# Expert stage of a diffusion step: a fourth split buffer for weights, laid in the token activations' tensors

## The chip, the core and the metric

The kernel runs on one core of a Trainium2 chip. The metric is the device time of one execution in microseconds (us). Five engines work side by side: TensorE (PE, matmuls), VectorE (DVE), ScalarE (ACT), GpSimd (POOL) and SyncE (SP, which issues most DMA transfers). They meet at semaphores.

## The reference, cut to what matters

The reference is one layer of a hybrid backbone on 640 tokens (128 of context, 512 latent) of width 1024. A mixer (a gated scan, differential attention and a merge) comes first; the change doesn't touch it. Then comes the expert stage, which is:

```
def ec_moe(h, router_w, w_gate, w_up, w_down):
    ...
    gate, idx = lax.top_k(jnp.swapaxes(aff, 1, 2), cap)
    ...
    a = jax.nn.silu(jnp.einsum('becd,edf->becf', xg, w_gate)) * jnp.einsum('becd,edf->becf', xg, w_up)
    y = jnp.einsum('becf,efd->becd', a, w_down) * gate[..., None].astype(h.dtype)
    return jnp.zeros_like(h).at[jnp.arange(B)[:, None], flat].add(y.reshape(B, N_EXPERTS * cap, D))
```

There are 16 experts. Each takes 80 tokens (64 latent and 16 of context) and three weight matrices of 1024 x 1024 in float32: gate, up and down. All weights are read once, 12.6 MB for an expert.

## The kernel before

To be exact enough, a product is made of three matmuls in a reduced float format (fp32r): both factors are split into a high part and a low part, and high x high, high x low and low x high are added (`mm3`, L1597 to L1601). ACT makes the high part by a copy with rounding, DVE the low part by a subtraction.

The expert stage runs from about 870 us to the end. Its weights come in pieces of 256 rows x 1024 columns, 1 MB, as 128 x 2048: four of gate, four of up and four of down for an expert, 192 in all, n = 0 to 191. The order is gate(e), up(e), down(e-1): the down product of an expert runs in the body of the next one. A piece goes through four steps:

- SP issues the transfer into one of six raw buffers (`eraw`, `NRE` = 6, `epiece`, L746). For piece n it waits until the low part of piece n-6 is made (`s_el`).
- ACT copies the raw piece into `Wh` (`ehi_first` L1067 at the start, `ehi_at` L1062 in the body, and again at the end, L1090). It waits for the landing (`s_er`) and for PE to be done with the piece that used the buffer before (`s_eu`). There are `NHL` = 3 buffers, so that is piece n-3. The body's step j handles piece n = 12e + j - 4.
- DVE makes `Wl` from the raw piece and `Wh` (`elo`, L1524).
- PE runs 12 matmuls on it, 80 rows of activations against 512 columns each (`piece_mm`, L1877), in the same order of pieces, and then raises `s_eu`.

Between the pieces other steps are written into each engine's program by hand, at fixed j. DVE: `alo` (low part of the hidden activations) after j = 3, `yout` (scaled output of the expert before) after 4, `xmod` (two operations on the gathered tokens) after 9, `xlo` (their low part) and `hidden` (silu(gate) x up) after 10. ACT: `ahi` after 3, `silu` after 7, `xhi` (high part of the gathered tokens) after 10. PE: transposition of the gathered tokens `turn_x` before 6, of the hidden ones `turn_a` after 11. POOL gathers the tokens of the next experts from HBM and scatters the outputs with an addition.

`act_hi` and `act_lo` are 128 x 8 x 640. They hold the split activations of all tokens for the layers ahead of the expert stage. In the expert stage slices 0, 1 and 2 of them hold the split activations of the experts (`xh`, `ah`, `xh1`); slices 3 to 7 are not used there.

Of the kernel before, what the change touches and what calls it, by code (L numbers as in the profile page):

```python
# [5 lines left out]
F32 = mybir.dt.float32  # L6
# [4 lines left out]
ALU = mybir.AluOpType  # L11
ACT = mybir.ActivationFunctionType
# [27 lines left out]
def fused_step(nc, A, outs):  # L40
# [8 lines left out]
    with ExitStack() as ctx:  # L49
# [155 lines left out]
        NRE = 6  # L205
        eraw = [part(0, 2048), part(2048, 2048), part(4096, 2048)] + raw
# [9 lines left out]
        brow = arena[:, o_vso + 2048:o_vso + 2560]  # L216
        yq = [v_hg, arena[:, o_vso + 2560:o_vso + 5120].rearrange("p (i n) -> p i n", i=NT)]
        kctx = yq[1][:, 0, :]

        xh, xl = (w[:, 0, :].rearrange("p (k t) -> p k t", k=KD) for w in (act_hi, act_lo))  # L220
        xh1, xl1 = (w[:, 2, :].rearrange("p (k t) -> p k t", k=KD) for w in (act_hi, act_lo))
# [636 lines left out]
        def _(act):  # L858
# [193 lines left out]
            def body(e, last=False):  # L1052
                for j in range(12):
                    ehi_at(e, j)
                    if j == 3:
                        ahi(e - 1)
                    if j == 7:
                        silu(e)
                    if j == 10 and not last:
                        xhi(e + 1)  # L1060

            def ehi_at(e, j):  # L1062
                act.wait_ge(s_er[(j + 2) % NRE], (e * 2 + (j - 4) // 6 + 1) * 16)
                act.wait_ge(s_eu, e * 12 + (j - 6))
                a.activation(Wh[(j + 2) % NHL], eraw[(j + 2) % NRE], ACT.Copy).then_inc(s_eh, 1)  # L1065

            def ehi_first(n):  # L1067
                act.wait_ge(s_er[n % NRE], 16 * (n // NRE + 1))
                if n >= NHL:
                    act.wait_ge(s_eu, n - 2)  # L1070
                a.activation(Wh[n % NHL], eraw[n % NRE], ACT.Copy).then_inc(s_eh, 1)

            filled(act, ("out", 1, NT - 1))
            for n in range(NHL):
                ehi_first(n)
            xhi(0)
            for n in range(NHL, 8):
                ehi_first(n)
                if n == 6:
                    act.wait_ge(s_eu, 4)  # L1080
                    a.activation(aa[0:CAP, :], pair(0)[0:CAP, :], ACT.Silu).then_inc(s_silu, 1)
# [4 lines left out]
            body(NE - 1, last=True)  # L1086
            for n in range(188, 192):
                act.wait_ge(s_er[n % NRE], 16 * (n // NRE + 1))
                act.wait_ge(s_eu, n - 2)
                a.activation(Wh[n % NHL], eraw[n % NRE], ACT.Copy).then_inc(s_eh, 1)  # L1090
                if n == 188:
                    ahi(NE - 1)

        @block.vector
        def _(dve):
# [427 lines left out]

            def elo(sl, ready, slot):  # L1524
                dve.wait_ge(s_eh, ready)
                v.tensor_tensor(Wl[sl], eraw[slot], Wh[sl].bitcast(F32), ALU.subtract).then_inc(s_el, 1)  # L1526

            def xmod(e):
                dve.wait_ge(s_xgT, e + 1)
# [24 lines left out]

            def body(e, first=False, second=False, last=False):
                for j in range(12):
                    elo((j + 2) % NHL, e * 12 + (j - 3), (j + 2) % NRE)
                    if j == 1 and first:
                        hidden(0, 8)
                    if j == 3:  # L1560
                        alo(e - 1)
                    if j == 4 and not first:
                        yout(e - 2, first=second)
                    if j == 9 and not last:
                        xmod(e + 1)
                    if j == 10:
                        if not last:
                            xlo(e + 1)
                        hidden(e, e * 12 + 4)

            for n in range(NHL):
                elo(n % NHL, n + 1, n % NRE)
            xmod(0)
            xlo(0)
            for n in range(NHL, 8):
                elo(n % NHL, n + 1, n % NRE)
                if n == 6:
                    xmod(1)
            xlo(1, (xh1, xl1))
# [2 lines left out]
            with dve.Fori(3, NE - 1) as e:  # L1582
                body(e)
            body(NE - 1, last=True)
            elo(188 % NHL, 189, 188 % NRE)
            alo(NE - 1)
            elo(189 % NHL, 190, 189 % NRE)
            yout(NE - 2)
            elo(190 % NHL, 191, 190 % NRE)
            elo(191 % NHL, 192, 191 % NRE)  # L1590
            yout(NE - 1)

        @block.tensor
        def _(pe):
# [282 lines left out]
            def piece_mm(pr, ready, sl, hi_, lo_, j):  # L1877

                pe.wait_ge(s_el, ready)
                wh, wl = (w[sl].rearrange("p (k n) -> p k n", k=2) for w in (Wh, Wl))  # L1880
# [13 lines left out]
            def body(e, first=False, last=False):  # L1894
                for j in range(12):
                    m, q = j // 4, j % 4
                    if j == 0:
                        pe.wait_ge(s_silu, e)
                    if j == 2 and first:
                        pe.wait_ge(s_xgm, 2)  # L1900
                        turn_a(0)
                    if j == 4:
                        pe.wait_ge(s_a, e)
                    if j == 6 and not last:
                        pe.wait_ge(s_alo, e)
                        turn_x(e + 1)
                    if j == 8:
                        pe.wait_ge(s_alo, e)
                        if not first:
                            pe.wait_ge(s_y, e - 1)  # L1910
                    hi_, lo_ = (ah, al) if m == 2 else (xh1, xl1) if first else (xh, xl)
                    if j == 0:
                        pe.wait_ge(s_xgl, e + 1)
                    piece_mm(m, e * 12 + (j - 3), (j + 2) % NHL, hi_, lo_, q)
                if not last:
                    pe.wait_ge(s_xgm, e + 2)
                turn_a(e)
# [2 lines left out]
            turn_x(0)  # L1920
            pe.wait_ge(s_xgl, 1)
            for n in range(8):
                piece_mm(n // 4, n + 1, n % NHL, xh, xl, n % 4)
                if n == 4:
                    pe.wait_ge(s_xgm, 1)
                    turn_x(1)
# [4 lines left out]
            pe.wait_ge(s_alo, NE)  # L1931
            pe.wait_ge(s_y, NE - 1)
            for q in range(4):
                piece_mm(2, 189 + q, (188 + q) % NHL, ah, al, q)


# [77 lines left out]
```

## Time and profile before

| | us |
|---|---|
| median of 3 runs | 1497.87 |
| lowest and highest | 1493.14 and 1497.9 |
| the profiled execution | 1495.61 |
| its span, first to last instruction | 1493.8 |

| engine | busy, us | share of the span |
|---|---|---|
| PE | 1346.1 | 90% |
| DVE | 1017.6 | 68% |
| ACT | 702.1 | 47% |
| POOL | 277.4 | 19% |

Over the whole span 296 MB are moved. The share of the sixteen DMA engines is low until about 870 us, and nine tenths or more in every slice of the expert stage but the last. Ends of matmuls are modelled in the profile, so starts are the better guide for PE: they are what the steps below use. A DMA share can be a little over 1, since packets on one engine overlap slightly.

### The profile page before, as it was taken

How to read it: one execution, taken by the hardware profiler on the slowest of the kernel's cores; microseconds unless marked ns; L12 is line 12 of the kernel's file. 1: busy time of each engine (PE TensorE's matmuls, PEld its weight loads, DVE VectorE, ACT ScalarE, POOL GpSimd, SP SyncE). 2: the span in 40 equal slices, each digit the busy share in tenths (PEclk: the TensorE clock that was granted, in tenths of full speed). 3: DMA queues.
4: the chain of work that ended last, by engine and by line, in shares of the span. 5: the costliest groups of instructions: out<-in, count | busy, mean ns of one | idle time of the engine just before them, and what ended most of it. 6: DMA issues, size and time to landing. Idle time of an engine off the chain costs nothing.

```text
span 1493.8 us, 18233 instructions
## 1 busy us (share of the span) xinstructions
PE 1346.1 (90%) x6820; PEld 1004.6 (67%) x6820; DVE 1017.6 (68%) x1093; ACT 702.1 (47%) x674; POOL 277.4 (19%) x193
## 2 busy tenths in 40 slices
PE   7788998888989978788999868999999999999995
PEld 1577887777979958684987725666666666666663
DVE  1766125444369868765443677899999898889993
ACT  2322234444335434314411125766667776767672
POOL 0022001111000000000000101144535335444222
PEclk9899999999989998878999878999999999999998
DMA  9412311113230121205415358999999999999992
GB/s 352 164 33 78 120 33 51 49 35 93 75 100 19 56 79 57 65 10 209 153 60 194 141 204 292 365 372 373 354 381 368 369 369 368 362 364 383 353 375 53
DMA packets 111843, 296.06 MB, mean 198 GB/s; under 512 B 7077, under 2 KB 33061, under 8 KB 111785
## 3 DMA queue, kind: packets, MB, share of 16 engines
q1 hardware_dynamic: 108264, 284.25, 52.4%
q0 software_dynamic: 3520, 11.01, 3.2%
q8 instruction: 39, 0.64, 0.2%
q14 instruction: 20, 0.16, 0.0%
HBM read 278.47 MB, written 16.78 MB: 198 GB/s over the span
## 4 chain that ended last, share of the span: by engine, by line
PE 67%; DVE 18%; issue 6%; ACT 6%; DMA 2%; POOL 1%; DVEq 0%; ACTq 0%; SPq 0%; POOLq 0%
PE ps L1599 17%; PE ps L1600 17%; PE ps L1601 17%; PE ps L1665 5%; PE ps L1775 3%; DVE w_lo L1526 3%; ACT w_hi L1065 2%; PE ps L1726 1%; ACT w_hi L876 1%; DVE arena L1542 1%; DMA arena<-in_w_mod_dram 1%; DVE arena L1166 1%; PE ps L1852 1%; DVE w_lo L1117 1%; DVE arena L1361 1%
## 5 line engine op out<-in xcount | busy, mean ns | idle before, releaser
L1526 DVE TENSOR_TENSOR w_lo<-arena,w_hi 128x2048 fp32r<-128x2048 f32 x192 | 435.3, 2287 | 65.1 <-ACT w_hi L1065 49.9
L1599 PE MATMUL ps<-w_hi,act_hi 128*80 128x512 f32 (+1 forms) x1048 | 418.9, 400 | 28.4 <-DVE w_lo L1526 15.0
L1600 PE MATMUL ps<-w_lo,act_hi 128*80 128x512 f32 (+1 forms) x1048 | 414.0, 395 | 0.0
L1601 PE MATMUL ps<-w_hi,act_lo 128*80 128x512 f32 (+1 forms) x1048 | 412.6, 394 | 0.0
L1065 ACT ACTIVATE w_hi<-arena 128x2048 fp32r<-128x2048 f32 x180 | 343.3, 1915 | 141.9 <-PE ps L1601 141.9
L1599 PEld LDWEIGHTS ps<-w_hi,act_hi 128*80 128x80 f32 (+1 forms) x1048 | 168.5, 161 | 115.3 <-DVE w_lo L1526 29.7
L1601 PEld LDWEIGHTS ps<-w_hi,act_lo 128*80 128x80 f32 (+1 forms) x1048 | 168.3, 161 | 75.4 <-issue 0.9
L1600 PEld LDWEIGHTS ps<-w_lo,act_hi 128*80 128x80 f32 (+1 forms) x1048 | 168.7, 161 | 68.6 <-issue 0.7
L1599 PE MATMUL ps<-act_hi,w_hi 128*128 128x320 f32 x576 | 190.6, 331 | 1.4 <-DVE w_lo L1117 0.7
L1600 PE MATMUL ps<-act_lo,w_hi 128*128 128x320 f32 x576 | 184.6, 321 | 0.0
L1601 PE MATMUL ps<-act_hi,w_lo 128*128 128x320 f32 x576 | 184.3, 320 | 0.0
L1117 DVE TENSOR_TENSOR w_lo<-arena,w_hi 128x2048 fp32r<-128x2048 f32 (+1 forms) x34 | 73.5, 2166 | 108.7 <-ACT w_hi L876 108.3
L880 ACT ACTIVATE arena<-ps 128x512 f32<-128x512 f32 (+3 forms) x84 | 51.4, 618 | 143.2 <-PE ps L1665 57.2
L1599 PEld LDWEIGHTS ps<-act_hi,w_hi 128*128 128x128 f32 x576 | 115.8, 201 | 3.7 <-issue 2.5
L839 POOL DMA_INDIRECT out_dram<-arena x16 | 73.1, 4567 | 228.3 <-DVE arena L1552 228.3
L1600 PEld LDWEIGHTS ps<-act_lo,w_hi 128*128 128x128 f32 x576 | 115.1, 200 | 0.0
L1601 PEld LDWEIGHTS ps<-act_hi,w_lo 128*128 128x128 f32 x576 | 114.2, 198 | 0.0
L1775 PE MATMUL ps<-arena 128*128 128x64 f32 x560 | 81.3, 311 | 33.6 <-DVE arena L1361 23.7
L793 POOL TENSOR_SCALAR arena<-arena 128x1 f32<-128x1 f32 (+2 forms) x44 | 9.8, 223 | 522.9 <-ACT arena L954 223.2
L1775 PEld LDWEIGHTS ps<-arena 128*128 128x128 f32 x560 | 79.4, 226 | 35.6 <-DVE arena L1361 24.6
L1665 PE MATMUL ps<-arena 128*2 128x512 f32 x192 | 90.6, 627 | 10.9 <-DMA arena<-in_w_mod_dram 10.1
L876 ACT ACTIVATE w_hi<-arena 128x2048 fp32r<-128x2048 f32 (+1 forms) x34 | 61.4, 1809 | 54.3 <-PE ps L1601 44.1
(199 smaller groups left out, 1351.1 us busy)
## 6 DMA issues: line engine op xcount, KB each, us to landing
arena<-in_w_exp_gate_dram SPq DMA_DIRECT2D x64, 1024.0 KB, 8.9
arena<-in_w_exp_up_dram SPq DMA_DIRECT2D x64, 1024.0 KB, 7.3
arena<-in_w_exp_down_dram SPq DMA_DIRECT2D x64, 1024.0 KB, 7.1
arena<-in_w_mod_dram SPq DMA_DIRECT2D x24, 1024.0 KB, 5.3
arena<-in_w_in_dram SPq DMA_DIRECT2D x18, 1024.0 KB, 5.3
arena<-in_w_in_dram SPq DMA_DIRECT2D x12, 512.0 KB, 5.5
gl_raw<-arena SPq DMA_DIRECT2D x32, 160.0 KB, 1.8
arena<-gl_raw SPq DMA_DIRECT2D x8, 640.0 KB, 10.2
```

What stands on the lines that cost most here:

```text
L839: g.indirect_dma_start(out=y_sample[0], out_offset=bass.IndirectOffsetOnAxis(ap=iscat[0:CAP_LAT, 0:1], axis=0), in_=ye[0:CAP_LAT, :], in_o ...
L876: a.activation(hl(key)[0][:, 0:w], rawv(key)[:, 0:w], ACT.Copy).then_inc(s_hi, 1)
L880: release(a.activation(dst, src, func, **kw), key)
L1065: a.activation(Wh[(j + 2) % NHL], eraw[(j + 2) % NRE], ACT.Copy).then_inc(s_eh, 1)
L1117: v.tensor_tensor(l_[:, 0:w], rawv(key)[:, 0:w], h_[:, 0:w].bitcast(F32), ALU.subtract).then_inc(s_lo, 1)
L1166: link(v.tensor_reduce(mx[:, m:m + 1], pair(m)[:, 0:nk], AX_X, ALU.max))
L1526: v.tensor_tensor(Wl[sl], eraw[slot], Wh[sl].bitcast(F32), ALU.subtract).then_inc(s_el, 1)
L1599: t.matmul(out, sh, mh, start=start, stop=False)
L1600: t.matmul(out, sh, ml, start=False, stop=False)
L1601: return t.matmul(out, sl, mh, start=False, stop=stop)
L1665: ins = t.matmul(bank(2 * modpair(j))[0:2, :], cond[:, kt, :], w[:, kk, :], start=kt == 0, stop=kt == 7)
L1775: ins = t.matmul(bank(4 + 2 * (lv % 2) + d)[:, 64 * c:64 * c + 64], KS[lv % 2][:, d, P * c:P * c + P], QC[lv % 2][:, d, 64 * c:64 * c + 64 ...
```

## The change

A fourth pair of split buffers is added for the expert stage. Its high part lies in slices 3 and on of `act_hi`, its low part in the same place of `act_lo`. The buffer of a piece is n modulo 4 instead of 3, and ACT waits for PE to be done with piece n-4 instead of n-3. To keep the order safe, `xhi` moves from step 10 to step 11 on ACT and `xlo` from step 10 to behind the split of step 11 on DVE. The layers ahead of the stage still use three buffers. Cut to its core:

```diff
+        NEW = 4
+        EWh, EWl = (ws + [a[:, 3:, :].rearrange("p k t -> p (k t)")[:, 0:2048]] for ws, a in ((Wh, act_hi), (Wl, act_lo)))
...
-                    if j == 10 and not last:
+                    if j == 11 and not last:
                         xhi(e + 1)
             def ehi_at(e, j):
                 act.wait_ge(s_er[(j + 2) % NRE], (e * 2 + (j - 4) // 6 + 1) * 16)
-                act.wait_ge(s_eu, e * 12 + (j - 6))
-                a.activation(Wh[(j + 2) % NHL], eraw[(j + 2) % NRE], ACT.Copy).then_inc(s_eh, 1)
+                act.wait_ge(s_eu, e * 12 + (j - 7))
+                a.activation(EWh[j % NEW], eraw[(j + 2) % NRE], ACT.Copy).then_inc(s_eh, 1)
             def ehi_first(n):
                 act.wait_ge(s_er[n % NRE], 16 * (n // NRE + 1))
-                if n >= NHL:
-                    act.wait_ge(s_eu, n - 2)
-                a.activation(Wh[n % NHL], eraw[n % NRE], ACT.Copy).then_inc(s_eh, 1)
+                if n >= NEW:
+                    act.wait_ge(s_eu, n - 3)
+                a.activation(EWh[n % NEW], eraw[n % NRE], ACT.Copy).then_inc(s_eh, 1)
...
             def body(e, first=False, second=False, last=False):
                 for j in range(12):
-                    elo((j + 2) % NHL, e * 12 + (j - 3), (j + 2) % NRE)
+                    elo(j % NEW, e * 12 + (j - 3), (j + 2) % NRE)
...
                     if j == 10:
-                        if not last:
-                            xlo(e + 1)
                         hidden(e, e * 12 + 4)
+                    if j == 11 and not last:
+                        xlo(e + 1)
...
-                    piece_mm(m, e * 12 + (j - 3), (j + 2) % NHL, hi_, lo_, q)
+                    piece_mm(m, e * 12 + (j - 3), j % NEW, hi_, lo_, q)
```

ACT at the start of the expert stage, before: the splits of pieces 0 to 5 and the high part of the first gathered tokens. The fourth split waits for PE (`s_eu`).

```order
L1071 ACTIVATE w_hi0<-arena 128x2048 [waits s_er0,psum_full2]
L1071 ACTIVATE w_hi1<-arena 128x2048 [waits s_er1]
L1071 ACTIVATE w_hi2<-arena 128x2048 [waits s_er2]
L1041 ACTIVATE act_hi<-arena 128x640 [waits s_xgf]
L1071 ACTIVATE w_hi0<-arena 128x2048 [waits s_eu,s_er3]
L1071 ACTIVATE w_hi1<-arena 128x2048 [waits s_eu,s_er4]
L1071 ACTIVATE w_hi2<-arena 128x2048 [waits s_eu,s_er5]
```

The same place with the change; `act_hi` with 128x2048 is the fourth buffer.

```order
L1074 ACTIVATE w_hi0<-arena 128x2048 [waits s_er0,psum_full2]
L1074 ACTIVATE w_hi1<-arena 128x2048 [waits s_er1]
L1074 ACTIVATE w_hi2<-arena 128x2048 [waits s_er2]
L1044 ACTIVATE act_hi<-arena 128x640 [waits s_xgf]
L1074 ACTIVATE act_hi<-arena 128x2048 [waits s_er3]
L1074 ACTIVATE w_hi0<-arena 128x2048 [waits s_eu,s_er4]
L1074 ACTIVATE w_hi1<-arena 128x2048 [waits s_eu,s_er5]
```

The fourth split now waits for its landing alone; from the fifth on each waits for PE, one piece further back than before.

DVE in the body of expert 2, steps 8 to 11, before: splits, `xmod` (the two rows on `arena` 128x640), `xlo` and `hidden` (80x1024).

```order
L1526 TENSOR_TENSOR w_lo1<-arena,w_hi1 128x2048 [waits s_eh]
L1526 TENSOR_TENSOR w_lo2<-arena,w_hi2 128x2048 [waits s_eh]
L1530 TENSOR_TENSOR arena<-ps,arena 128x640 [waits s_xgT]
L1532 TENSOR_TENSOR arena<-arena 128x640 [waits s_xgm]
L1526 TENSOR_TENSOR w_lo0<-arena,w_hi0 128x2048 [waits s_eh,s_xgf]
L1537 TENSOR_TENSOR act_lo<-arena,act_hi 128x640 [waits s_xgh]
L1542 TENSOR_TENSOR arena<-arena,ps 80x1024 [waits s_eu,s_silu]
L1526 TENSOR_TENSOR w_lo1<-arena,w_hi1 128x2048 [waits s_eh]
```

The same place with the change.

```order
L1529 TENSOR_TENSOR w_lo0<-arena,w_hi0 128x2048 [waits s_eh]
L1529 TENSOR_TENSOR w_lo1<-arena,w_hi1 128x2048 [waits s_eh]
L1533 TENSOR_TENSOR arena<-ps,arena 128x640 [waits s_xgT]
L1535 TENSOR_TENSOR arena<-arena 128x640 [waits s_xgm]
L1529 TENSOR_TENSOR w_lo2<-arena,w_hi2 128x2048 [waits s_eh,s_xgf]
L1545 TENSOR_TENSOR arena<-arena,ps 80x1024 [waits s_eu,s_silu]
L1529 TENSOR_TENSOR act_lo<-arena,act_hi 128x2048 [waits s_eh]
L1540 TENSOR_TENSOR act_lo<-arena,act_hi 128x640 [waits s_xgh]
```

The low part of the gathered tokens (128x640) moved from ahead of `hidden` to behind the last split.

## Rows read from the trace of the kernel before

**Rows 1.** List of waits from 900 us on: engine, line, releaser, us, times, longest.

```profile
ACT w_hi L1065 <- PE ps L1601: 141.9, 135, 2.2
PE ps L1599 <- DVE w_lo L1526: 15.0, 15, 1.1
```

**Rows 2.** Timeline of PE in one expert: start, duration, engine, line, operation, idle before.

```profile
1098.53 0.39 PE L1601 MATMUL ps<-w_hi,act_lo 128*80 128x512 f32 x1
1099.02 0.47 PE L1599 MATMUL ps<-w_hi,act_hi 128*80 128x512 f32 x1
...
1101.39 0.39 PE L1600 MATMUL ps<-w_lo,act_hi 128*80 128x512 f32 x1
1101.62 0.40 PE L1601 MATMUL ps<-w_hi,act_lo 128*80 128x512 f32 x1
1103.09 0.46 PE L1599 MATMUL ps<-w_hi,act_hi 128*80 128x512 f32 x1 [1.07 <-DVE w_lo L1526]
```

**Rows 3.** Timeline of DVE over the same stretch.

```profile
1092.67 2.29 DVE L1526 TENSOR_TENSOR w_lo<-arena,w_hi 128x2048 fp32r<-128x2048 f32 x1 [1.03 <-ACT w_hi L1065]
1094.88 0.82 DVE L1530 TENSOR_TENSOR arena<-ps,arena 128x640 f32<-128x640 f32 x1
1095.73 0.83 DVE L1532 TENSOR_TENSOR arena<-arena 128x640 f32<-128x640 f32 x1
1096.68 2.29 DVE L1526 TENSOR_TENSOR w_lo<-arena,w_hi 128x2048 fp32r<-128x2048 f32 x1
1098.88 0.82 DVE L1537 TENSOR_TENSOR act_lo<-arena,act_hi 128x640 fp32r<-128x640 f32 x1
1099.62 1.21 DVE L1542 TENSOR_TENSOR arena<-arena,ps 80x1024 f32<-80x1024 f32 x1
1100.75 6.68 DVE L1526 TENSOR_TENSOR w_lo<-arena,w_hi 128x2048 fp32r<-128x2048 f32 x3
```

**Rows 4.** Timeline of ACT at the start of the stage.

```profile
901.01 0.74 ACT L1041 ACTIVATE act_hi<-arena 128x640 fp32r<-128x640 f32 x1 [6.21 <-DVE arena L1532]
907.12 1.91 ACT L1071 ACTIVATE w_hi<-arena 128x2048 fp32r<-128x2048 f32 x1 [5.37 <-PE ps L1601]
```

**Rows 5.** Stretches: length, busy PE, PEld, DVE, ACT, POOL, PE clock, DMA share, GB/s.

```profile
905.00:914.00 9.00, 9.00 (x40) 5.79 (x39) 4.46 (x2) 5.19 (x3) 0.00 (x0) 0.97 0.20 50
1122.36:1158.19 35.83, 34.68 (x162) 22.19 (x161) 32.31 (x18) 24.92 (x16) 17.77 (x7) 1.00 1.01 371
1167.00:1172.00 5.00, 4.85 (x22) 2.91 (x21) 4.84 (x5) 3.78 (x4) 3.28 (x4) 1.00 1.03 422
1464.00:1476.00 12.00, 7.13 (x25) 4.52 (x26) 6.58 (x5) 4.97 (x3) 4.02 (x2) 0.72 0.20 27
```

**Rows 6.** DMA queues and issues, 943.2 to 1444.8 (14 experts): share; us to landing.

```profile
q1 hardware_dynamic: 45729, 176.29, 93.8%
q0 software_dynamic: 2704, 8.52, 7.3%
...
arena<-in_w_exp_down_dram SPq DMA_DIRECT2D x57, 1024.0 KB, 7.1
arena<-in_w_exp_gate_dram SPq DMA_DIRECT2D x56, 1024.0 KB, 9.0
```

**Rows 7.** DMA queues, 874 to 882, weights alone: packets, MB, share.

```profile
q1 hardware_dynamic: 918, 3.31, 102.9%
```

**Rows 8.** The transfer of piece 9 on SP's queue: issue, and time to landing.

```profile
L748 SPq DMA_DIRECT2D arena<-in_w_exp_gate_dram x1: 383/383/383, 911.5 to 911.5; - x1
...
DMA to landing us min/median/max: 4.8/4.8/4.8
```

**Rows 9.** The transfer of piece 187, the same view.

```profile
L748 SPq DMA_DIRECT2D arena<-in_w_exp_down_dram x1: 373/373/373, 1442.7 to 1442.7; - x1
...
DMA to landing us min/median/max: 6.0/6.0/6.0
```

**Rows 10.** Timeline of PE: first matmul of piece 187, and of piece 188.

```profile
1459.26 0.39 PE L1599 MATMUL ps<-w_hi,act_hi 128*80 128x512 f32 x1
...
1468.87 0.69 PE L1599 MATMUL ps<-w_hi,act_hi 128*80 128x512 f32 x1 [6.16 <-issue]
```

More of the change, by code:

```diff
@@ L1063, in ehi_at @@
                 act.wait_ge(s_er[(j + 2) % NRE], (e * 2 + (j - 4) // 6 + 1) * 16)
-                act.wait_ge(s_eu, e * 12 + (j - 6))
-                a.activation(Wh[(j + 2) % NHL], eraw[(j + 2) % NRE], ACT.Copy).then_inc(s_eh, 1)
+                act.wait_ge(s_eu, e * 12 + (j - 7))
+                a.activation(EWh[j % NEW], eraw[(j + 2) % NRE], ACT.Copy).then_inc(s_eh, 1)
             def ehi_first(n):
                 act.wait_ge(s_er[n % NRE], 16 * (n // NRE + 1))
-                if n >= NHL:
-                    act.wait_ge(s_eu, n - 2)
-                a.activation(Wh[n % NHL], eraw[n % NRE], ACT.Copy).then_inc(s_eh, 1)
+                if n >= NEW:
+                    act.wait_ge(s_eu, n - 3)
+                a.activation(EWh[n % NEW], eraw[n % NRE], ACT.Copy).then_inc(s_eh, 1)
             filled(act, ("out", 1, NT - 1))
-            for n in range(NHL):
+            for n in range(3):
                 ehi_first(n)
             xhi(0)
-            for n in range(NHL, 8):
+            for n in range(3, 8):
                 ehi_first(n)
@@ L1088, in _ @@
                 act.wait_ge(s_er[n % NRE], 16 * (n // NRE + 1))
-                act.wait_ge(s_eu, n - 2)
-                a.activation(Wh[n % NHL], eraw[n % NRE], ACT.Copy).then_inc(s_eh, 1)
+                act.wait_ge(s_eu, n - 3)
+                a.activation(EWh[n % NEW], eraw[n % NRE], ACT.Copy).then_inc(s_eh, 1)
                 if n == 188:
@@ L1525, in elo @@
                 dve.wait_ge(s_eh, ready)
-                v.tensor_tensor(Wl[sl], eraw[slot], Wh[sl].bitcast(F32), ALU.subtract).then_inc(s_el, 1)
+                v.tensor_tensor(EWl[sl], eraw[slot], EWh[sl].bitcast(F32), ALU.subtract).then_inc(s_el, 1)
             def xmod(e):
@@ L1566, in body @@
                     if j == 10:
-                        if not last:
-                            xlo(e + 1)
                         hidden(e, e * 12 + 4)
-            for n in range(NHL):
-                elo(n % NHL, n + 1, n % NRE)
+                    if j == 11 and not last:
+                        xlo(e + 1)
+            for n in range(3):
+                elo(n % NEW, n + 1, n % NRE)
             xmod(0)
             xlo(0)
-            for n in range(NHL, 8):
-                elo(n % NHL, n + 1, n % NRE)
+            for n in range(3, 8):
+                elo(n % NEW, n + 1, n % NRE)
                 if n == 6:
@@ L1584, in _ @@
             body(NE - 1, last=True)
-            elo(188 % NHL, 189, 188 % NRE)
+            elo(188 % NEW, 189, 188 % NRE)
             alo(NE - 1)
-            elo(189 % NHL, 190, 189 % NRE)
+            elo(189 % NEW, 190, 189 % NRE)
             yout(NE - 2)
-            elo(190 % NHL, 191, 190 % NRE)
-            elo(191 % NHL, 192, 191 % NRE)
+            elo(190 % NEW, 191, 190 % NRE)
+            elo(191 % NEW, 192, 191 % NRE)
             yout(NE - 1)
@@ L1879, in piece_mm @@
                 pe.wait_ge(s_el, ready)
-                wh, wl = (w[sl].rearrange("p (k n) -> p k n", k=2) for w in (Wh, Wl))
+                wh, wl = (w[sl].rearrange("p (k n) -> p k n", k=2) for w in (EWh, EWl))
                 for kk in range(2):
@@ L1922, in _ @@
             for n in range(8):
-                piece_mm(n // 4, n + 1, n % NHL, xh, xl, n % 4)
+                piece_mm(n // 4, n + 1, n % NEW, xh, xl, n % 4)
                 if n == 4:
@@ L1933, in _ @@
             for q in range(4):
-                piece_mm(2, 189 + q, (188 + q) % NHL, ah, al, q)
+                piece_mm(2, 189 + q, (188 + q) % NEW, ah, al, q)
 _INS = ['x_prompt', 'x_sample', 'cache_v', 'state_hgrn', 'w_mod', 'b_mod', 'w_in', 'diff_lambda', 'w_branch_hgrn', 'w_branch_attn', 'w_out', 'router_w', 'w_exp_gate', 'w_exp_up', 'w_exp_down']
```

## The prediction

> **What bounds the kernel now.** I read the list of waits first, then the timelines of TensorE (PE), VectorE (DVE) and ScalarE (ACT) in one expert, then the DMA shares, because the edit touches only the expert stage. A piece below is 1 MB of expert weights (256 x 1024), numbered n = 0 to 191, twelve to an expert.
>
> The waits [rows 1] say that ACT's split waits for PE 135 times, 141.9 us in all: it wants a buffer that PE still reads. That is idle time of an engine with time to spare. What counts is the other row: PE's first matmul of a piece waited for DVE's low part 15 times, 15.0 us, longest 1.1. Fourteen of these are one hole per expert. [Rows 2] show it: matmuls start 0.23 us apart (1101.39, 1101.62), then the next at 1103.09, which is 1.47 - 0.23 = 1.24 us lost. One piece earlier the step is 0.49 (1098.53 to 1099.02), 0.26 lost. So a hole costs 1.24 + 0.26 = **1.50 us per expert**.
>
> [Rows 3] show who is late. DVE has between three splits of 2.2 to 2.3 us each the gather's modulation (0.82 + 0.83), the low part of the activations (0.82) and the hidden product (1.21), some 3.5 us. PE takes 2.75 us for a piece. With three buffers ACT may start piece n when PE ends n-3, two pieces before it is wanted: 2 x 2.75 = 5.5 us, of which ACT's 1.91 [rows 4] and DVE's 2.29 take 4.2. The lead is 1.3 us, and the burst eats it.
>
> One expert lasts 35.83 us (the window of [rows 5]), so PE alone could do it in 35.83 - 1.50 = **34.33**. DVE is busy 32.31 of it, ACT 24.92.
>
> The third thing to see is the DMA. In that window its share is 1.01 at 371 GB/s; over 14 experts, 501.6 us, the two queues took 93.8% + 7.3% = 101.1% of 16 engines [rows 6]. Where weights alone stream with a full queue, the share is 102.9% [rows 7] and the rate 422 GB/s [rows 5]. So the engines are idle only (102.9 - 101.1)/102.9 = 1.75% of the time, 0.63 us of an expert. Gathers and scatters take the rest. **The DMA can't do an expert in less than about 35.20 us.** That is the term that decides the size here: the hole is 1.50, but only 0.63 of it can be had for ever.
>
> **The change part by part.**
>
> Fourth buffer. ACT may start n when PE ends n-4; the lead is 1.3 + 2.75 = 4.0 us. The burst needs about 3.5 less what DVE gains per piece (2.75 - 2.2, twice), 2.4 at most. The hole goes: at most 14 x 1.50 = 21.0 us. The number of splits, matmuls and transfers is unchanged. The transfers' ring of six raw buffers is the same too, but each transfer is issued when a low part is done, so it goes out up to one piece earlier.
>
> Low part of the activations moved behind the last split of the expert (0.82 us), on ACT its high part likewise. It leaves the path to the late split; the next reader is PE's first piece of the next expert, behind one more piece and a transposition. The cover is over 2.75 us. I count nothing extra, it is within the 1.50. If the cover were gone it would cost 0.8 per expert.
>
> Start of the stage. ACT is free at 901.01 + 0.74 = 901.75 and then waits 5.37 us for PE, until 907.12 [rows 4]. Piece 3 now needs no such wait: its low part ends at 901.75 + 1.91 + 2.29 = 906.0, and the transfer of piece 9 goes out then rather than at 911.5 [rows 8]. The DMA is nearly idle here (share 0.20 from 905 to 914 [rows 5]). Piece 4 still waits for PE's first piece at 907.12 and is done about 911.4, where piece 3 was. So from there all transfers are one piece ahead: the DMA has **2.5 us** of work done sooner (1 MB at 422 GB/s [rows 5]). PE itself gains nothing here.
>
> DMA idle. With one more piece queued its pauses should close: 14 x 0.63 = **8.8 us** at most, zero at least.
>
> Stock. Weights land earlier than needed today. Piece 187, the last ahead of the closing four, was issued at 1442.7, landed 6.0 us later at 1448.7 [rows 9], and PE began it at 1459.26 [rows 10]: 10.55 us. The least is 1.91 + 2.29 + 0.1 for hand-offs, 4.3, plus up to 1.2 for the hidden product in front and about 0.6 for uneven landings, 6.0. PE can move **4.5 us** (3.5 to 6.2) towards the landings before it must wait for them.
>
> Tail. After piece 187 PE waits 6.16 us [rows 10] for the scaled output of the expert before, which DVE makes after a split that ACT starts only after the last activations' high part. That order is unchanged, so nothing there: 0.
>
> Buffer 4 lies in another tensor. No row shows a split or a matmul on it. Splits of the same shape into the three others take 1.91 and 2.29; I take the same and 0 for it. The nearest row on that tensor is the 128x640 copy into `act_hi`, 0.74 us [rows 4]; scaled by columns that would be 2.4 for a split, 0.5 more on every fourth piece. ACT, busy 24.92 of 35.83, hides that, and less than nothing isn't to be had where the engines are not the bound.
>
> **Sum.** 2.5 + 8.8 + 4.5 = **15.8 us**, below the 21.0 of PE, so DMA decides. Against the profiled execution's 1495.61 (span 1493.8) that is 1479.8; against the median 1497.87, 1482.1. I say 1482. Seen in time: PE gains 1.50 an expert while DMA gives 0.63, so the stock of 2.5 + 4.5 lasts 7.0/0.87 = 8 experts, and the last six come at 35.2.
>
> **Rivals.**
>
> *DMA keeps up with PE.* If its share can rise further, or gathers and scatters cost less when hidden, the whole 21 goes: 1497.9 - 21 = 1477. For it: no wait for a landing appears in [rows 1]. Against it: the share of 1.01.
>
> *DMA gives no more than today.* If the 1.75% can't be closed, since a piece lands only when the slowest of 16 engines is done, only 2.5 + 4.5 = 7 is left: 1491. For it: the queue already holds more than one transfer most of the time (7.1 to 9.0 us to land [rows 6] against 4.8 for a lone one [rows 8]).
> The Trainium skill, page DMA: Bandwidth & Descriptors, section Where 436 GB/s comes from, speaks for this rival: it says that loads from HBM are bound near 358 GB/s a core and that the vendor's model uses 368. By that figure the present 371 would be the ceiling and the last two terms of this rival's case the whole gain; the trace differs from it with 422 in a quiet stretch, so I don't take it.
>
> *The buffer doesn't help.* The burst is DVE's own and DVE is at 32.31 of 34.33 us. If hand-offs add 2 us an expert, DVE is the bound and the hole only moves: 1498, within 0.3%. Against: DVE's gaps outside the burst all end on ACT.
>
> *Slower: the clock.* Once DMA decides, PE waits in lumps behind the scatters and gathers. After 1.07 us idle the granted clock stayed 1.00 [rows 2, 5]; after 6.16 it was 0.72 over 12 us [rows 5, 10]. That is half level (1.2 instead of 2.4 GHz) for 0.28/0.5 x 12 = 6.7 us, 4.9 of them idle, so at least 0.9 us lost by a fall, 2.7 (a whole piece at half speed) at most. Two falls an expert at 1.8 make 34.33 + 3.6 = 37.9, 2.1 above today: 1498 + 14 x 2.1 = 1527. It decides from where falls cost more than the 1.50 of the hole. Lumps of more than about 3 us would be needed, and a scatter delays a landing by some 2.
>
> **How the numbers follow.** Forecast (DMA-bound, 13 to 19 gained) 52%; DMA keeps up 16%; DMA as today 18%; no help 9%; slower 5%. The range takes in the first three, with 3 us below and above for the spread of the medians (1493.1 to 1497.9): 1474 to 1493. About 4.5 us, 0.3%, is what a measurement can tell from no change. Faster than that: 52 + 16 + 15 of the 18 = 83%; same 12%; slower 5%.
>
> **What would show it.** The row of PE waiting for DVE's low part once per expert is gone in the first experts. The expert period is near 34.4 first and 35.2 later. ACT's split waits for the DMA in the later half, which it never does now. DMA share goes from 1.01 to about 1.03, GB/s from 371 to about 378. Piece 9 is issued at about 906. The 6.16 us before the last four pieces stays. I am wrong if the period is 34.4 to the end, if it stays near 35.8 with the holes elsewhere, or if the PE clock falls inside the stage.

## The result, and the profile after

The changed kernel takes 1471.45 us in the median of 4 runs (1469.97 to 1473.77). The kernel before, run beside it, takes 1495.64 (1493.14 to 1497.9). The ratio is 0.9843, with a 95% interval of 0.983 to 0.9856. That is faster, as forecast, but by 10 us more than the 1482 of the prediction, and below the low end of its range, 1474. The profiled execution took 1470.25 with a span of 1468.4; before it was 1495.61 and 1493.8. So 25.4 us are to be found.

First the list of waits of PE from 900 us on, after (engine, line, releaser, us in total, times, longest). The row of [rows 1] in which PE waited 15 times for DVE's low part has no successor.

```profile
PE ps L1602 <- issue: 6.2, 1, 6.2
PE ps L1602 <- DVE act_lo L1540: 3.5, 1, 3.5
```

Of the other engines in the same view of after, ACT waits for PE less long than the 141.9 us of [rows 1] (94.0 + 36.2, split over the two kinds of buffer). No row has ACT waiting for a weight's landing.

```profile
ACT w_hi L1068 <- PE ps L1604: 94.0, 114, 1.4
...
ACT act_hi L1068 <- PE ps L1604: 36.2, 44, 0.9
DVE w_lo L1529 <- ACT w_hi L1068: 17.5, 43, 1.0
```

The period of an expert tells the rest. Two stretches of one expert each, after, in the columns of [rows 5] (length, busy PE, PEld, DVE, ACT, POOL, PE clock, DMA share, GB/s):

```profile
972.50:1006.66 34.16, 34.16 (x162) 22.39 (x161) 32.31 (x18) 25.04 (x16) 20.44 (x7) 1.00 1.03 394
1040.82:1074.98 34.16, 34.16 (x162) 22.39 (x161) 32.31 (x18) 25.04 (x16) 20.20 (x7) 1.00 1.02 385
```

PE is busy for the whole of both. The period is 34.16 us from the first repeated expert to the last, against 35.83 before, so 1.67 less, and 14 of these make 23.4 us. DVE's and ACT's work is what it was, 32.31 and 25.04 (24.92). The DMA moves the same bytes in less time, at 385 to 394 GB/s where it was 371.

The DMA queues of after over 14 experts (packets, MB, share of 16 engines), and the median time to landing, against [rows 6]:

```profile
q1 hardware_dynamic: 45896, 176.97, 94.8%
q0 software_dynamic: 2704, 8.52, 7.6%
...
arena<-in_w_exp_down_dram SPq DMA_DIRECT2D x58, 1024.0 KB, 7.7
arena<-in_w_exp_gate_dram SPq DMA_DIRECT2D x56, 1024.0 KB, 8.8
```

Start and end of the stage on PE's timeline. The first row is of before; the others are of after and answer to [rows 10].

```profile
902.73 0.72 PE L1599 MATMUL ps<-w_hi,act_hi 128*80 128x512 f32 x1 [3.47 <-DVE act_lo L1537]
```

```profile
900.82 0.71 PE L1602 MATMUL ps<-w_hi,act_hi 128*80 128x512 f32 x1 [3.47 <-DVE act_lo L1540]
...
1436.64 0.72 PE L1894 MATMUL ps<-arena 80*128 80x80 f32 x8
1443.52 0.68 PE L1602 MATMUL ps<-w_hi,act_hi 128*80 128x512 f32 x1 [6.16 <-issue]
```

The whole account closes on these rows. From the first piece to piece 188 it was 1468.87 - 902.73 = 566.14 us, and is 1443.52 - 900.82 = 542.70: 23.4 less. The stage starts 1.9 us earlier, and that is spread and no effect of the change: in the thirteen traces on record this first matmul starts anywhere from 900.47 (experiment 3) to 904.26 (experiment 6). From piece 188 to the end it is 24.88 after and 24.93 before. 23.4 + 1.9 + 0.05 = 25.4.

### The profile page after: what moved, and what is told of

It is laid out like the page before. It is cut to its first block, busy times and chain, and to the rows that moved or that the text cites. A ratio compares the mean times of both kernels' runs of the same rounds, so it can differ in the third digit from the quotient of the medians.

```text
span 1468.4 us, 18232 instructions
## 1 busy us (share of the span) xinstructions
PE 1336.2 (91%) x6820; PEld 1005.8 (68%) x6820; DVE 1017.2 (69%) x1093; ACT 702.9 (48%) x674; POOL 339.7 (23%) x193
## 4 chain that ended last, share of the span: by engine, by line
PE 78%; DVE 12%; ACT 4%; issue 3%; DMA 2%; POOL 1%; DVEq 0%; ACTq 0%; SPq 0%; POOLq 0%
PE ps L1602 21%; PE ps L1603 20%; PE ps L1604 20%; PE ps L1668 5%; PE ps L1778 4%; ACT w_hi L879 1%; PE ps L1729 1%; DMA arena<-in_w_mod_dram 1%; DVE arena L1169 1%; PE ps L1855 1%; DVE w_lo L1120 1%; DVE arena L1364 1%; DVE arena L1363 1%; ACT arena L883 1%; DVE arena L1220 1%
## 5 line engine op out<-in xcount | busy, mean ns | idle before, releaser
L1602 PE MATMUL ps<-w_hi,act_hi 128*80 128x512 f32 (+1 forms) x856 | 341.6, 399 | 12.0 <-issue 6.2
L1529 DVE TENSOR_TENSOR w_lo<-arena,w_hi 128x2048 fp32r<-128x2048 f32 x144 | 325.4, 2286 | 24.4 <-ACT w_hi L1068 17.5
L1603 PE MATMUL ps<-w_lo,act_hi 128*80 128x512 f32 (+1 forms) x856 | 338.8, 396 | 0.0
L1604 PE MATMUL ps<-w_hi,act_lo 128*80 128x512 f32 (+1 forms) x856 | 337.4, 394 | 0.0
L1068 ACT ACTIVATE w_hi<-arena 128x2048 fp32r<-128x2048 f32 x135 | 258.5, 1918 | 94.0 <-PE ps L1604 94.0
L1602 PEld LDWEIGHTS ps<-w_hi,act_hi 128*80 128x80 f32 (+1 forms) x856 | 140.2, 164 | 71.6 <-issue 8.6
L1604 PEld LDWEIGHTS ps<-w_hi,act_lo 128*80 128x80 f32 (+1 forms) x856 | 139.8, 163 | 59.6 <-issue 0.7
L1603 PEld LDWEIGHTS ps<-w_lo,act_hi 128*80 128x80 f32 (+1 forms) x856 | 140.3, 164 | 55.7 <-issue 0.7
L1529 DVE TENSOR_TENSOR act_lo<-arena,act_hi 128x2048 fp32r<-128x2048 f32 x48 | 109.8, 2288 | 8.3 <-ACT act_hi L1068 6.1
L1778 PE MATMUL ps<-arena 128*128 128x64 f32 x560 | 81.3, 311 | 33.6 <-DVE arena L1364 23.7
L1068 ACT ACTIVATE act_hi<-arena 128x2048 fp32r<-128x2048 f32 x45 | 86.3, 1918 | 36.2 <-PE ps L1604 36.2
```

The source lines that it names most:

```text
L1068: a.activation(EWh[j % NEW], eraw[(j + 2) % NRE], ACT.Copy).then_inc(s_eh, 1)
L1529: v.tensor_tensor(EWl[sl], eraw[slot], EWh[sl].bitcast(F32), ALU.subtract).then_inc(s_el, 1)
L1602: t.matmul(out, sh, mh, start=start, stop=False)
L1603: t.matmul(out, sh, ml, start=False, stop=False)
L1604: return t.matmul(out, sl, mh, start=False, stop=stop)
L1778: ins = t.matmul(bank(4 + 2 * (lv % 2) + d)[:, 64 * c:64 * c + 64], KS[lv % 2][:, d, P * c:P * c + P], QC[lv % 2][:, d, 64 * c:64 * c + 64 ...
```

## The experiments

**1. The order alone, with three buffers.** The gathered tokens' split moved behind the last one, the fourth buffer left out. Against the changed kernel:

```diff
-        NEW = 4
-        EWh, EWl = (ws + [a[:, 3:, :].rearrange("p k t -> p (k t)")[:, 0:2048]] for ws, a in ((Wh, act_hi), (Wl, act_lo)))
...
-                act.wait_ge(s_eu, e * 12 + (j - 7))
-                a.activation(EWh[j % NEW], eraw[(j + 2) % NRE], ACT.Copy).then_inc(s_eh, 1)
+                act.wait_ge(s_eu, e * 12 + (j - 6))
+                a.activation(Wh[(j + 2) % NHL], eraw[(j + 2) % NRE], ACT.Copy).then_inc(s_eh, 1)
```

> Three split buffers as before, but the order of the change: the high part of the gathered tokens at step 11 on ScalarE, their low part behind the last split on VectorE. Theory L (the hole is VectorE's burst less the lead of the split buffers, and nothing else limits): the burst shrinks by the 0.74 us of the low part, so the expert takes 35.83 - 0.74 = 35.1 us and the kernel gains 14 x 0.74 = 10 us. Rival M (the gain of the change comes from transfers going out a piece earlier): nothing is issued earlier here, so gain near 0.

Measured: 1483.7 us, ratio 0.9924 (0.9909 to 0.9939), period 35.07. PE's wait for the low part and the window of one expert:

```profile
PE ps L1599 <- DVE w_lo L1526: 4.6, 14, 0.3
```

```profile
1048.90:1083.90 35.00, 34.57 (x161) 22.23 (x160) 32.15 (x19) 25.02 (x16) 19.98 (x7) 1.00 1.01 376
```

The gain is 10.9 us where theory L had 10. The holes are still 14, but of 0.3 us each instead of 1.07. Taking 0.82 us of DVE work out of the burst gives 0.76 of the 1.67 us per expert. So with three buffers the moved low part is worth nearly half of what the change brought, and the prediction had named no price for it apart from the buffer.

**2. Four buffers, old order.** The split of the gathered tokens back to its old place, with a wait that keeps the shared tensor safe:

```diff
-                    if j == 11 and not last:
+                    if j == 10 and not last:
+                        act.wait_ge(s_eu, e * 12 + 4)
```

> Four split buffers, with the order of before (high part of the gathered tokens at step 10, with a wait of its own for TensorE's step 7, and their low part ahead of the hidden product). Theory L: the lead is 1.3 + 2.75 = 4.0 us against a burst that cost 2.9 to 3.0 (lead 1.3 plus hole 1.67), so no hole: expert 34.16 us, the same time as the changed kernel, ratio 0.984 to before. Rival O (the new order matters as well): an expert between 34.2 and 34.9.

Measured: 1472.17, ratio 0.9843 (0.9827 to 0.9858), the same as the change. Its window of one expert:

```profile
1042.00:1076.16 34.16, 34.16 (x162) 22.39 (x161) 32.31 (x19) 25.05 (x15) 20.37 (x7) 1.00 1.03 391
```

This is theory L again. The buffer by itself closes the hole, and the order then adds nothing. The two parts of the change are two cures for one burst; their gains don't add.

**3. A longer burst.** Two more DVE operations on 128x640 (0.82 us each) per expert, behind the hidden product. They write to slices that nothing reads.

```diff
+                        for w in (act_lo, act_hi):
+                            v.tensor_tensor(w[:, 7, :].rearrange("p (k t) -> p k t", k=KD), xgt3, xgt3, ALU.subtract)
```

> The changed kernel with two more VectorE operations of 128x640 (about 0.8 us each, results unused) between the hidden product and the last split of each expert. Theory L: the lead has 4.0 - (2.97 - 0.74) = 1.8 us to spare, the addition is 1.5 to 1.65, VectorE's load rises from 32.3 to 33.9 of 34.16: no or hardly any hole (under 0.2 us), ratio 0.984 to 0.986. Rival V (VectorE as a whole becomes the bound, hand-offs included): expert over 34.5 us, ratio 0.988 or more.

Measured: 1526.16, ratio 1.0221 (1.0191 to 1.025), so 55 us slower than the change for some 25 us of added DVE work. This was a clear miss, and none of my theories had a place for it. Most experts still take 33.6 to 35.0 us, but five of them take 43.2 to 46.4. What these five and the expert behind each take above 34.16 adds up to 54.6 us, nearly the whole loss. PE's wait in those is not for DVE but for the gather:

```profile
PE ps L1879 <- DMA arena<-xn_rows,arena: 43.7, 5, 9.7
```

These waits are 43.7 us of the loss. Most of the rest is the clock: behind each wait the matmuls of 512 columns take 0.63 us for a time instead of 0.39.

The gather is late because of POOL, which ahead of each indirect DMA copies a column of indices (80, 64 and 16 numbers). POOL's timeline in one bad expert, and DVE's at its end:

```profile
1066.19 24.30 POOL L837 COPY arena<-arena 64x1 uint32 x1
1090.44 0.18 POOL L838 COPY arena<-arena 16x1 uint32 x1
...
1101.84 22.80 POOL L831 COPY arena<-arena 80x1 uint32 x1 [5.14 <-DMA out_dram<-arena]
```

```profile
1083.76 4.48 DVE L1529 TENSOR_TENSOR w_lo<-arena,w_hi 128x2048 fp32r<-128x2048 f32 x2
1088.16 2.28 DVE L1529 TENSOR_TENSOR act_lo<-arena,act_hi 128x2048 fp32r<-128x2048 f32 x1
1090.49 2.29 DVE L1529 TENSOR_TENSOR w_lo<-arena,w_hi 128x2048 fp32r<-128x2048 f32 x1
```

A copy of 64 numbers took 24.30 us and ended when DVE ended: 1088.16 + 2.28 = 1090.44. From 1066.4 to there each DVE instruction begins before the recorded end of the one before; the first gap is 1090.44 to 1090.49. Then the copy of 16 numbers takes 0.18 us. Four of the five late gathers stand behind a copy at L831 of 22.6 to 22.8 us that ends at such a gap. The fifth doesn't: its copy took 1.91 us, and the indirect DMA instruction itself was slow.

```profile
1292.94 25.01 POOL L826 DMA_INDIRECT arena<-xn_rows,arena  x1 [0.85 <-POOL arena L831]
```

I overlooked that row before experiment 4. Experiments 4 and 5 test this reading. In experiment 7, where DVE has little to do, no copy of L831 takes more than 0.18:

```profile
L831 POOL COPY arena<-arena x15: 177/180/181, 898.5 to 1335.4; 80x1 uint32 x13, 80x1 uint32<-80x1 uint32 x2
```

**4. The same burst without the index copies.** The indirect DMAs read their column of the index table directly, in a POOL loop written out:

```diff
-                g.tensor_copy(icur[0:CAP, 0:1], iT[0:CAP, bass.ds(e, 1)]).then_inc(s_icp, 1)
-                pool.wait_ge(s_icp, e + 1)
...
-                                     in_offset=bass.IndirectOffsetOnAxis(ap=icur[0:CAP, 0:1], axis=0)).then_inc(s_gath, 16)
+                                     in_offset=bass.IndirectOffsetOnAxis(ap=iT[0:CAP, e:e + 1], axis=0)).then_inc(s_gath, 16)
```

> The kernel e3_burst_plus (two more VectorE operations per expert) without GpSimd's copies of the indices: its loop over experts is written out, and each gather and scatter takes its index column directly. Theory G (GpSimd's small copy can't finish while VectorE runs without a gap; the gather then goes out up to 24 us late and TensorE waits for it, five times 10 us): without the copies no wait for a gather is left and the time falls from 1526 to about 1472 to 1478 (expert 34.2 to 34.5). Rival V (VectorE's load as such, 33.9 of 34.16 us, is the cause): the time stays above 1510.

Measured: 1487.01 in the median of 10 runs, nine of them from 1481.46 to 1494.5 and one at 1511.93; ratio of the nine 0.9946 (0.9924 to 0.9968). Against experiment 3 that is 39 us back, and waits for the gather fall from five to one. In the profiled execution (1482.41) the rest is the same delay at another place. POOL's timeline, and a window of 350 us of the same kernel:

```profile
988.59 23.66 POOL L826 DMA_INDIRECT arena<-xn_rows,arena  x1 [4.94 <-DMA out_dram<-arena]
```

```profile
1040.00:1390.00 350.00, 350.00 (x1638) 229.31 (x1637) 342.94 (x205) 256.33 (x155) 107.28 (x30) 1.00 1.02 386
```

Here the indirect DMA instruction itself took 23.66 us, as the one at 1292.94 in experiment 3; the other fifteen gathers of this kernel take 0.90 to 2.11. It costs one expert 10.0 us, and the stage starts 2.0 later than in the profiled execution of the change: 12.0 of the 12.2 us between them. The window shows DVE busy 98% with no hole on PE at all: DVE's load as such is not what cost the time. The expectation of full recovery was wrong by 9 to 15 us. Whether the slower of the ten executions held more such delays isn't shown, since only one was profiled.

The Trainium skill, page SBUF — State Buffer, section SBUF: two separate sides, says that a VectorE instruction with two SBUF inputs and a GpSimd instruction that reads SBUF share a pair of ports as an exclusive lock, held for the whole instruction by whoever starts first. The direction agrees. The trace of experiment 3 shows more than one instruction's worth: the copy of 24.30 us stood through some fifteen DVE instructions in a row, two of which (L1549, L1555) take one input from PSUM, and was let in at a gap of 0.05 us.

**5. One added operation instead of two.**

> The changed kernel with one more VectorE operation (0.74 to 0.82 us) per expert in place of two, GpSimd's copies kept. Asks how near the edge the changed kernel is: VectorE still has gaps adding up to about 1.0 us an expert. Theory G: some gap is left after the burst, copies take 10 to 20 us but the gather still lands before TensorE wants it (it has 18 to 21 us to spare): ratio to before 0.984 to 0.986. If the copies already miss every gap: over 0.99.

Measured: 1471.04, ratio 0.9833 (0.9817 to 0.985), the same as the change. The copies at L837 now take up to 12.8 us where in the change they take up to 9.9, and before up to 7.7. The row of before, of after, and of this run (duration in ns: least, median, most):

```profile
L834 POOL COPY arena<-arena x16: 193/1942/7689, 949.3 to 1476.3; 64x1 uint32 x13, 64x1 uint32<-64x1 uint32 x3
```

```profile
L837 POOL COPY arena<-arena x16: 180/1576/9890, 947.7 to 1453.0; 64x1 uint32 x13, 64x1 uint32<-64x1 uint32 x3
```

```profile
L837 POOL COPY arena<-arena x16: 177/1819/12829, 949.4 to 1454.8; 64x1 uint32 x13, 64x1 uint32<-64x1 uint32 x3
```

The longest copy of 16 numbers, at L838, goes from 0.8 (before) and 10.7 (the change) to 13.7. PE waits for none of them yet. These copies end otherwise than in experiment 3. The one of 13.65 us ends at 1068.09, with the end of a DVE split (1068.06) and without a gap behind it; ten more do the same at this place.

```profile
1054.44 13.65 POOL L838 COPY arena<-arena 16x1 uint32 x1
```

```profile
1065.78 2.28 DVE L1529 TENSOR_TENSOR act_lo<-arena,act_hi 128x2048 fp32r<-128x2048 f32 x1
1067.98 0.81 DVE L1549 TENSOR_TENSOR act_lo<-ps,act_hi 128x640 fp32r<-128x640 f32 x1
```

So a recorded gap is not the only way in. Why the copies of experiment 3 stood through the same place stays open.

The edge lies between one and two added operations. With one, DVE is busy 32.87 us of 34.16 and nothing is lost; with two it is 33.47 (342.94 of 350 in the window of experiment 4) and the time is. The change itself stands between one and two such operations from it. In its trace one gather had already become late: the indirect DMA instruction took 10.61 us, and 7.3 us were left before PE wanted the tokens, where the gathers of the other experts from the fourth on leave 18 to 21.

**6 to 8. The floor of the DMA.** To see what an expert costs when PE and DVE have little to do, only the high x high matmuls remain (a third of them), and DVE subtracts a quarter of each piece. Against the change (the same edit on the kernel before gives experiment 6):

```diff
-                v.tensor_tensor(EWl[sl], eraw[slot], EWh[sl].bitcast(F32), ALU.subtract).then_inc(s_el, 1)
+                v.tensor_tensor(EWl[sl][:, 0:512], eraw[slot][:, 0:512], EWh[sl][:, 0:512].bitcast(F32), ALU.subtract).then_inc(s_el, 1)
...
-                        ins = mm3(bank(2 * pr + b)[0:CAP, :], (hi_[:, kt, :], lo_[:, kt, :]), (wh[:, kk, cs], wl[:, kk, cs]), kt == 0, kt == 7)
+                        ins = t.matmul(bank(2 * pr + b)[0:CAP, :], hi_[:, kt, :], wh[:, kk, cs], start=kt == 0, stop=kt == 7)
```

Experiment 6, three buffers:

> The kernel before (three buffers), with computation left out so that the transfers are what remains: TensorE multiplies high by high only (a third of the expert matmuls) and VectorE subtracts a quarter of each piece. All transfers, gathers and scatters stay. Theory D (as predicted: the DMA needs 35.2 us for an expert): the expert stays at 35.2 or more. Theory P (packet time is elastic, the share of 1.01 is no bound): the expert falls below 34.16, to between 30.5 (12 pieces at 2.54) and 33.5, and the DMA is then the bound.

Experiment 7, four buffers:

> The changed kernel with the same computation left out as in the run before. If the fourth buffer changes how fast the DMA can go, the expert is shorter than there; if the DMA's floor doesn't depend on it, both have the same period within 0.3 us. Theory D: 35.2 in both. Theory P: 30.5 to 33.5 in both.

Experiment 8, as 7 but without the two scatters of an expert and the waits for them (DVE's and SP's waits go too, and aren't shown):

```diff
-                g.indirect_dma_start(out=y_sample[0], out_offset=bass.IndirectOffsetOnAxis(ap=iscat[0:CAP_LAT, 0:1], axis=0),
-                                     in_=ye[0:CAP_LAT, :], in_offset=None, compute_op=ALU.add).then_inc(s_scat, 16)
...
-                pool.wait_ge(s_scat, 32 * e + 32)
```

> As the run before, and the scatters of the experts' outputs are left out too (32 transfers). Gathers stay. The period falls by what the two scatters of an expert cost the weight transfers. From the trace before, landings beside scatters come about 2.5 us later than otherwise: expected 2 to 2.6 us less than the run before, and a DMA rate near 410 GB/s.

Measured, one run each: 1441.2, 1437.56 and 1409.73 us, with periods of 33.57, 33.57 and 32.17. The queues of the three kernels from 940 to 1360 us, in that order:

```profile
q1 hardware_dynamic: 40911, 157.74, 94.9%
q0 software_dynamic: 2538, 7.97, 7.9%
```

```profile
q1 hardware_dynamic: 40946, 157.87, 95.0%
q0 software_dynamic: 2496, 7.87, 7.8%
```

```profile
q1 hardware_dynamic: 42742, 164.79, 99.5%
q0 software_dynamic: 1152, 3.93, 3.2%
```

Here the DMA is the bound: now ACT's splits do wait for landings (first row, experiment 7), and DVE is far from full in the window of one expert (second).

```profile
ACT w_hi L1068 <- DMA arena<-in_w_exp_gate_dram: 31.4, 40, 1.4
```

```profile
1100.00:1133.57 33.57, 22.65 (x66) 11.04 (x65) 13.68 (x18) 24.95 (x15) 4.53 (x6) 0.65 1.03 394
```

So the floor is 33.57 us per expert with three buffers or with four, where the prediction had 35.20 and theory P, just missed, at most 33.5. PE at 34.16 lies above it by 0.59, and PE decides. The scatters cost 33.57 - 32.17 = 1.4 us per expert of DMA time; I had expected 2 to 2.6, and 410 GB/s where 402 came.

**9. The tail.** The 6.16 us before piece 188 had been counted as unchanged. In this version the scaled output of the expert before, and the split of piece 189, stand ahead of the last activations' split:

```diff
-                if n == 188:
+                if n == 189:
...
-            alo(NE - 1)
...
+            alo(NE - 1)
```

> The changed kernel with another order at the end: VectorE makes the scaled output of expert 14 before the low part of the last activations, and ScalarE splits piece 189 before their high part. TensorE waits 6.16 us ahead of the last four pieces today. Expected: this falls to about 2 us (scaled output 1.3, low part 0.8), and the slow start after it (4.33 us for a piece instead of 2.75) may go too: 4 to 6 us less than the changed kernel, ratio to before 0.980 to 0.9815. Rival: something else ends last there, a gain under 1 us.

Measured: 1467.04, ratio 0.9811 (0.9798 to 0.9825), as expected. PE's wait falls from 6.16 to 1.65:

```profile
1438.15 0.72 PE L1894 MATMUL ps<-arena 80*128 80x80 f32 x8
1440.52 0.46 PE L1602 MATMUL ps<-w_hi,act_hi 128*80 128x512 f32 x1 [1.65 <-DVE act_lo L1549]
1440.82 0.46 PE L1603 MATMUL ps<-w_lo,act_hi 128*80 128x512 f32 x1
1441.08 0.63 PE L1604 MATMUL ps<-w_hi,act_lo 128*80 128x512 f32 x1
```

The matmuls still slow down, from 0.39 to 0.63 us, after a wait of only 1.65 that follows eight small transpositions. (In experiment 11 they don't, after the same wait.)

**10. The tail, with PE kept at work.** Experiment 9 with eight matmuls of 512 columns, whose result nothing reads, between the transpositions and piece 188:

```diff
+            for q in range(8):
+                t.matmul(bank(0)[0:CAP, :], xh[:, q, :], act_hi[:, 7, 0:512], start=q == 0, stop=q == 7)
```

> e4_tail with eight more matmuls of 512 columns on TensorE (result unused, 1.8 us in all) between the last transposition and the last four pieces, where it is idle for 1.86 us and where the first of the four pieces then takes 4.4 us instead of 2.75. If the idle time is what lowers the granted clock there: the piece takes 2.75 us and the kernel gains 1.5 us on e4_tail, ratio to before near 0.980. Rival: the clock falls anyway, same time as e4_tail or 0.1 us more.

Measured: 1466.19 (1464.81 to 1466.49), ratio 0.9803 (0.979 to 0.9816). The stretch of 12 us in after, experiment 9 and this one:

```profile
1437.00:1449.00 12.00, 5.84 (x24) 3.66 (x22) 8.71 (x5) 6.10 (x4) 4.79 (x1) 0.72 0.00 0
```

```profile
1437.00:1449.00 12.00, 10.35 (x44) 6.60 (x43) 6.74 (x5) 4.30 (x3) 4.47 (x4) 0.86 0.21 27
```

```profile
1437.00:1449.00 12.00, 12.00 (x59) 7.85 (x58) 7.39 (x5) 4.31 (x3) 4.47 (x4) 1.00 0.21 27
```

The granted clock stays 1.00 and piece 188 takes 2.8 us instead of 4.4. From its first matmul to the end of the span it is 23.5 us instead of 25.2. The median gains only 0.85 us over experiment 9, within both intervals, so in the time it is not settled. That the added matmuls are the cause isn't shown either: the clock stays up without them in experiment 11. It is the fastest of the kernels that compute everything.

**11. The tail without index copies.** Experiment 9 together with the edit of experiment 4.

> e4_tail and no index copies on GpSimd. The copies take up to 10.7 us there but the gathers land 18 to 21 us before they are wanted, so nothing waits for them: same time as e4_tail, ratio to before 0.981 within its interval, perhaps 0.3 us at the very end, where a scatter's copies stand ahead of the scatter. Rival: indirect transfers themselves are slower with a strided index column, which would show as a longer GpSimd instruction but not in the time.

Measured: 1467.22, ratio 0.9809 (0.9794 to 0.9824), the same as experiment 9. In this kernel the copies cost nothing. Its trace bears on experiments 9 and 10: PE waits the same 1.65 us behind the same transpositions, with nothing put in, and the granted clock stays 1.00.

```profile
1441.76 0.46 PE L1593 MATMUL ps<-w_hi,act_hi 128*80 128x512 f32 x1 [1.65 <-DVE act_lo L1540]
1442.06 0.39 PE L1594 MATMUL ps<-w_lo,act_hi 128*80 128x512 f32 x1
```

```profile
1437.00:1449.00 12.00, 10.35 (x52) 6.76 (x51) 7.98 (x5) 4.31 (x3) 4.20 (x2) 1.00 0.22 27
```

From piece 188 to the end it is 23.4 us here, as in experiment 10. In both profiled executions the stretch from piece 0 to piece 188 is 1.4 us longer than in experiment 9, so the whole time hardly shows it.

## Why the prediction was wrong

**The hole.** Right in kind: it was the short lead over DVE's burst, as experiments 1 and 2 show from both sides. One reading was loose: the steps between DVE's splits add up to 0.82 + 0.83 + 0.82 + 1.21 = 3.68 us, not 3.5, which leaves the need (2.6 with it) below the lead of 4.0 all the same. The hole's size was put at 1.50 and is 1.67. The stops have an after-effect that I left out. In before the matmul behind each of the two stops gives way to the next only after 0.30 us, where the others take 0.23, so twice 0.07 more. The one of [rows 2] that starts at 1099.02 is followed by:

```profile
1099.32 0.39 PE L1600 MATMUL ps<-w_lo,act_hi 128*80 128x512 f32 x1
```

Over 14 experts this term was 2.4 us short. The rest, 1.67 - 1.64, is rounding.

**The DMA's floor.** This is the step that failed: "The DMA can't do an expert in less than about 35.20 us." I took the share for a load and divided it by the highest share seen. But the time that packets are charged with is not fixed. Share times period should then be the same in all kernels, and it falls: 101.1% of 35.83 is 36.2 us before, 101.8% of 35.07 is 35.7 in experiment 1, 102.4% of 34.16 is 35.0 after, 102.8% of 33.57 is 34.5 at the floor. One weight packet took on average 0.938 x 501.6 x 16/45729 = 0.165 us before, 0.158 after, 0.156 at the floor. The shares of 1.01 said that some transfer was nearly always under way. They did not say that it could go no faster. The GB/s beside them hinted that it could: 371 against 422 in a quiet stretch [rows 5]; at the floor it was 394. What the runs showed in place of the 35.20 is a floor of 33.57, below PE's 34.16. So PE decides to the end, with an expert at 34.16 throughout: one of the signs of being wrong that the prediction had named.

**Head start, DMA idle, stock.** These three terms, 2.5 + 8.8 + 4.5, were to be summed only if the DMA decided. It did not, so none was drawn on, and the full gain of PE's side holds. Head start happened as described: piece 9's transfer went out at 904.1, and with the stage 1.9 us earlier that is the 906.0 of the sum. It answers to [rows 8]:

```profile
L751 SPq DMA_DIRECT2D arena<-in_w_exp_gate_dram x1: 382/382/382, 904.1 to 904.1; - x1
```

**The account of the miss.** 21.0 - 15.8 = 5.2 us withheld for the DMA, 2.4 for the hole, 1.9 for the earlier start of the stage: 9.5, which is 1479.8 - 1470.3 of the profiled executions. The 1.9 is spread and tells nothing of the mechanism. Between the medians, 1482 and 1471.45, another 2.2 us lie in the kernel before: the prediction took its 1497.87 of three runs, and beside the change it was 1495.64.

**The moved low part.** "Nothing extra" holds with four buffers (experiment 2). With three the move alone gains 0.76 us per expert (experiment 1).

**Buffer 4 and the tail.** Both zeros were right. A split into the fourth buffer takes 2.288 us on DVE against 2.286 for the others, one on ACT 1.918 in either, and the 6.16 us wait stayed. DVE's two groups of after:

```profile
L1529 DVE TENSOR_TENSOR w_lo<-arena,w_hi 128x2048 fp32r<-128x2048 f32 x144 | 325.4, 2286 | 24.4 <-ACT w_hi L1068 17.5
L1529 DVE TENSOR_TENSOR act_lo<-arena,act_hi 128x2048 fp32r<-128x2048 f32 x48 | 109.8, 2288 | 8.3 <-ACT act_hi L1068 6.1
```

**The rivals.** What came was the first, "DMA keeps up with PE", at 16% and 1477; its 21.0 was short by the same 2.4 of the hole. What I had against it, the share of 1.01, was the misreading above; what I had for it, that no engine waited for a landing, was the better evidence. "DMA gives no more than today" fell at 385 to 394 GB/s. Of the sentence cited there: the Trainium skill, page DMA: Bandwidth & Descriptors, section Where 436 GB/s comes from, has loads from HBM bound near 358 GB/s, half of what two cores share, and the runs here, on one core, held 388 over 14 experts and 402 without scatters, so the measurement decides against it. "The buffer doesn't help" fell with the waits. The clock rival didn't occur in the stage (1.00 in both windows). Its condition of lumps of some 3 us isn't settled by the runs: a stop of 1.65 us behind transpositions was followed by the lower clock in experiment 9 and not in experiment 11, and the 1.07 of [rows 2] amid large matmuls was not.

**Chances.** DVE at 32.31 of 34.16 us was taken as the danger of the fourth rival, in which hand-offs make DVE the bound. Experiments 3 to 5 show that a danger was near, by another mechanism and between one and two operations off.

**What stays open.** Why a weight packet takes longer where less is queued: a transfer of 1 MB landed 7.6 us after its issue before (median of the stage), 8.1 after, 13.9 at the floor, where the packets were shortest. Why the time of experiment 4 spreads over 30 us. What lets a GpSimd copy in where DVE shows no gap. And why the clock fell behind the 1.65 us in one trace and not in another.

## What to carry to other kernels

A DMA share above 1.0 says that a transfer is nearly always under way, not that the rate is at its end: look at the GB/s against the best stretch, at who waits for a landing, and if it decides the sum, measure the floor with the compute cut away. When a buffer more and a shorter burst both cure one stall, cost them together, since the gains overlap. Before an engine is filled to its last per cent, see which other engine it can hold off, and how long the work behind that one can wait.

## What the runs showed of the hardware

- While VectorE ran fifteen instructions without a gap, a GpSimd copy of 64 numbers took 24.30 us (0.18 at the least) and ended at the first gap, of 0.05 us (experiment 3). An indirect DMA instruction took 25.01 and 23.66 us in the same way (experiments 3 and 4; 0.90 to 2.11 for the other gathers of 4). Copies of 12.8 to 13.7 us ended with a VectorE instruction but without a gap (experiment 5). With VectorE busy 32.87 us of 34.16 nothing was late for TensorE; at 33.47 the kernel lost 55 us with the copies, 16 without.
- The mean packet of the weight stream took from 0.165 us down to 0.156 as the demand rose, and the rate went from 371 to 394 GB/s beside gathers and scatters and to 402 without the scatters, at a share of 1.01 to 1.03 throughout.
- Two indirect scatters with add per expert cost the stream 1.4 us.
- After 1.65 us without a matmul, behind eight small transpositions, the clock granted to TensorE fell to its lower level in experiment 9 (1.2 GHz; the matmul of 512 columns from 0.39 to 0.63 us, from 1441.08 on, back at 2.4 GHz by 1444.46) and stayed at 2.4 GHz in experiment 11, and in experiment 10 with matmuls put in. After the five waits of 7.4 to 9.7 us in experiment 3 it fell each time.
